# Sparse heads in pairs, values in column halves, early mixer tiles, and three group sums on GpSimd

## What is computed

```
o_sb  = stick_breaking_attention(q_sb, k_sb, v_sb)          # 8 heads
o_dsa = dsa_attention(q_dsa, k_dsa, v_dsa, q_ix, k_ix, w_ix)
        # top 128 keys per query from index scores -> mask
        # p = softmax(q k^T * d^-0.5 + mask), o = p v; k and v are shared by the 8 heads
o = concatenate([o_sb, o_dsa]) @ w_out
x = layer_norm(ALPHA * x + (1 + g_m) * o)
mod = silu(c) @ w_mod + b_mod     # 2 layers x 6 x 1024 columns, in groups of 512 columns
```

## Time and profile before

| | us |
|---|---|
| median of 3 runs | 1759.19 (1757.92 to 1764.79) |
| the profiled execution | 1757.3 |
| its span | 1755.5 |
| PE busy | 1652.4 (94%) |
| DVE busy | 1009.7 (58%) |
| ACT busy | 658.4 (38%) |
| POOL busy | 323.7 (18%) |
| mean granted PE clock | 0.979 |

### The profile page before, as it was taken

How to read it: one execution, slowest core, us unless ns; L and a number is a source line. 1 busy time by engine, 2 the same in 40 slices (tenths; PEclk the granted TensorE clock), 3 DMA queues, 4 the chain that set the end, 5 groups by cost and what they waited for, 6 DMA issues and landing times.

```text
span 1755.5 us, 22795 instructions
## 1 busy us (share of the span) xinstructions
PE 1652.4 (94%) x8957; PEld 1360.5 (77%) x8957; DVE 1009.7 (58%) x1435; ACT 658.4 (38%) x887; POOL 323.7 (18%) x250
## 2 busy tenths in 40 slices
PE   4999999999999997999999999899979899999999
PEld 3798787888777875788887887677757588888887
DVE  3568798777868758533333446757576723333243
ACT  4323465442264523422332123434463533333121
POOL 0000000000000003788885011224301000000011
PEclk8999999999999999999999999999999999999999
DMA  7645200352210332556554332221102133332421
GB/s 277 212 144 192 96 3 1 115 168 96 96 49 25 97 117 97 157 181 189 179 182 160 114 104 79 77 68 64 34 25 75 65 100 96 96 96 90 133 86 48
DMA packets 145606, 187.93 MB, mean 107 GB/s; under 512 B 7054, under 2 KB 104566, under 8 KB 145525
## 3 DMA queue, kind: packets, MB, share of 16 engines
q1 hardware_dynamic: 145524, 186.82, 33.2%
HBM read 184.70 MB, written 2.10 MB: 106 GB/s over the span
## 4 chain that ended last, share of the span: by engine, by line
PE 62%; DVE 13%; POOL 9%; issue 6%; DMA 5%; ACT 3%; SPq 1%; POOLq 0%; DVEq 0%; ACTq 0%
PE ps L841 7%; PE ps L842 7%; PE ps L843 7%; POOL mraw L628 4%; POOL msum L635 4%; DMA mraw<-in_w_mod_dram 3%; PE ps L1343 2%; PE ps L1351 2%; PE ps L1344 2%; PE ps L1347 2%; PE ps L1350 2%; PE ps L1352 2%; PE ps L1406 2%; PE ps L1408 2%; PE ps L1407 2%
## 5 line engine op out<-in xcount | busy, mean ns | idle before, releaser
L1538 ACT ACTIVATE whi<-wraw 128x2048 fp32r<-128x2048 f32 x71 | 135.8, 1913 | 306.3 <-PE ps L843 210.2
L2053 DVE TENSOR_TENSOR wlo<-wraw,whi 128x2048 fp32r<-128x2048 f32 x64 | 148.2, 2315 | 150.6 <-ACT whi L1538 150.4
L2810 DVE TENSOR_TENSOR wlo<-wraw,whi 128x2048 fp32r<-128x2048 f32 x22 | 51.6, 2347 | 204.2 <-ACT whi L1902 204.2
L1343 PE MATMUL ps<-uH,whi 128*128 128x512 f32 x352 | 140.1, 398 | 10.6 <-ACT uH L1870 8.3
L1344 PE MATMUL ps<-uH,wlo 128*128 128x512 f32 x352 | 138.9, 394 | 0.0
L841 PE MATMUL ps<-hH,whi 128*128 128x512 f32 x352 | 138.8, 394 | 0.0
L843 PE MATMUL ps<-hH,wlo 128*128 128x512 f32 x352 | 137.7, 391 | 0.0
L842 PE MATMUL ps<-hL,whi 128*128 128x512 f32 x352 | 137.5, 391 | 0.0
L1350 PE MATMUL ps<-uH,whi 128*128 128x512 f32 x352 | 136.9, 389 | 0.0
L1352 PE MATMUL ps<-uH,wlo 128*128 128x512 f32 x352 | 136.9, 389 | 0.0
L1351 PE MATMUL ps<-uL,whi 128*128 128x512 f32 x352 | 136.9, 389 | 0.0
(11 more groups left out here) (500 smaller groups left out, 3828.8 us busy)
## 6 DMA issues: line engine op xcount, KB each, us to landing
mraw<-in_w_mod_dram SPq DMA_DIRECT2D x104, 512.0 KB, 3.8
wraw<-in_w_gate_dram SPq DMA_DIRECT2D x22, 1024.0 KB, 5.3
wraw<-in_w_up_dram SPq DMA_DIRECT2D x22, 1024.0 KB, 5.4
wraw<-in_w_down_dram SPq DMA_DIRECT2D x16, 1024.0 KB, 5.1
wraw<-in_w_in_dram SPq DMA_DIRECT2D x11, 1024.0 KB, 5.5
mfirst<-in_w_mod_dram SPq DMA_DIRECT2D x16, 512.0 KB, 7.6
wraw<-in_w_in_even_dram SPq DMA_DIRECT2D x8, 1024.0 KB, 5.1
wraw<-in_w_in_odd_dram SPq DMA_DIRECT2D x16, 512.0 KB, 4.6
```

Of the source, the lines that this page charges most:

```text
L1343: mm(o[m], w_[0][m][:, k], uH[:, k], start=(k == 0), stop=False)
L2053: V.tensor_tensor(wlo[:, n % 2, :], wraw[:, n % 2, :], whi[:, n % 2, :].bitcast(F32), ALU.subtract).then_inc(lo_done, 1)
```

## The change

The items run in pairs of heads: item i now has pair `p = i // 8`, query block `q = i // 2 % 4` and head `e = i % 2` of the pair. The turned exponentials of a whole pair are kept, and the values are made once per pair with the values stationary (64 columns) and the exponentials moving, head 0 into partitions 0 to 63 and head 1 into 64 to 127 of one bank. The result lies already turned. The row sums' reciprocals are therefore spread to rows and turned by PE (`factor_rows`), copied by ACT (`factor_copy`) and multiplied in by DVE (`sparse_out`). The four tiles of the stick-breaking heads are turned and split between items. Items with q even are moved by DVE, others by ACT. POOL sums groups 14 to 16. Group 14 is turned after item 14, 15 after 25, 16 in the second chunk of the projection, and with it `sum_group(17)` moves. `sb_values(7)` stands before the wait for the masks.

```
-DSA_TURN = {11: 14, 23: 15}
-DSA_JOB = {2: 1, 8: 2, 14: 3}
-OUT_TURN = {0: 16}
+DSA_TURN = {14: 14, 25: 15}
+DSA_JOB = {2: 1, 8: 2, 17: 3}
+OUT_TURN = {1: 16}
+MIX_TILES = (0, 1, 2, 3, 4, 5, 6, 7)
+SB_TILE = {3: 0, 5: 1, 6: 2, 9: 3}
+TILE_BANK = (2, 7, 2, 7)
+R_TILE = {12: 0, 20: 1, 28: 2}
-G_DVE = (*range(10, 18), 29)
+G_DVE = (10, 11, 12, 13, 17, 29)
...
+        ptdT, = overlay([("ptdT", [P, 2, 2, 13, P], F32)])
...
+            pool.wait_ge(zero_rd, 8)
+            pool.wait_ge(msk_rd, 3)
+            for g_ in range(14, 17):
+                pool.wait_ge(modT, g_)
+                for kp in range(4):
+                    pool.wait_ge(m_landed[kp % 2], 16 * (2 * (g_ - 4) + kp // 2 + 1))
+                    sum_tick(kp, kp % 2, msum_at(g_))
...
-            def dsa_values(i):
-                h, q = i // 4, i % 4
-                pe.wait_ge(dpt_rd[i % 2], i // 2 + 1)
-                if q == 0 and h >= 2:
-                    pe.wait_ge(do_rd, h - 1)
-                for c in range(q + 1):
-                    last = mm(ps[:, 2 + 5 * (h % 2), q * HD:q * HD + HD], ptdT[:, i % 2, c * P:c * P + P],
-                              T0[:, c, DSV:DSV + HD], start=(c == 0), stop=(c == q))
-                last.then_inc(dpv_rd, 1)
+            def dsa_values(p, cs):
+                if cs[0] == 0:
+                    for e in range(2):
+                        pe.wait_ge(dpt_rd[e], 4 * p + 4)
+                    if p < 2:
+                        pe.wait_ge(ao_lo, mixed(2 + p))
+                    else:
+                        pe.wait_ge(do_rd, p - 1)
+                for c in cs:
+                    for e in range(2):
+                        last = mm(ps[e * HD:e * HD + HD, 2 + 5 * (p % 2), c * P:SEQ], T0[:, c, DSV:DSV + HD],
+                                  ptdT[:, p % 2, e, 4 * c:3 * c + 4, :].rearrange("p b n -> p (b n)"),
+                                  start=(c == 0), stop=(c == 3), skip_group_check=True)
...
+            def factor_rows(p):
+                bank = 0 if p == 3 else 3
+                pe.wait_ge(rows_rd, p + 1)
...
+                for q in range(TT):
+                    last = tr(ps[:, bank, q * P:q * P + P], rows_of[:, q * P:q * P + P], ident[:])
+                last.then_inc(aoT, 1)
             pe.wait_ge(wgt_rd, NH - 1)
             dsa_scores(0)
+            dsa_scores(1)
+            sb_values(NH - 1)
             pe.wait_ge(msk_rd, 3)
-            dsa_scores(1)
             dsa_scores(2)
-            sb_values(NH - 1)
-            pe.wait_ge(so_rd, NH)
             for i in range(NS):
                 dsa_turn(i)
+                if i == 2:
+                    pe.wait_ge(so_rd, NH)
                 if i in DSA_JOB:
                     dsa_job(9 + DSA_JOB[i])
                 if i + 3 < NS:
                     dsa_scores(i + 3)
-                if i >= 1:
-                    dsa_values(i - 1)
+                if i >= 8 and i % 8 == 0:
+                    dsa_values(i // 8 - 1, (0, 1, 2, 3))
+                if i in SB_TILE:
+                    sb_tile(SB_TILE[i])
+                if i in R_TILE:
+                    factor_rows(R_TILE[i])
                 if i in DSA_TURN:
-                    pe.wait_ge(job_lo, 10 + sum(at < i for at in DSA_JOB))
+                    pe.wait_ge(fac_copied, 1 if DSA_TURN[i] == 14 else 2)
                     turn_group(DSA_TURN[i])
-            dsa_values(NS - 1)
+            factor_rows(3)
+            dsa_values(3, (0, 1, 2, 3))
...
-            pe.wait_ge(do_rd, NH)
-            mixer_out(0, T0)
             out_product(0, 0, NC1 + 10)
...
             dsa_max(0)
             dsa_max(1)
+            sb_out(NH - 1)
             dsa_max(2)
-            sb_out(NH - 1)
             for i in range(NS):
-                if i % 2 == 0:
+                if on_vector(i):
                     dsa_move(i)
-                if i in DSA_JOB:
-                    dsa_low(DSA_JOB[i])
                 if i + 3 < NS:
                     dsa_max(i + 3)
-                if i >= 4 and i % 4 == 1:
-                    dsa_out(i // 4 - 1)
+                if i - 1 in SB_TILE:
+                    sb_tile_low(SB_TILE[i - 1])
+                if i - 1 in DSA_JOB:
+                    dsa_low(DSA_JOB[i - 1])
+                if i >= 8 and i % 8 == 0:
+                    sum_rows(i // 8 - 1)
+                if i - 1 in R_TILE:
+                    sparse_out(R_TILE[i - 1])
+                if i - 3 in R_TILE:
+                    sparse_low(R_TILE[i - 3])
                 if i - 1 in DSA_TURN:
                     group_columns(DSA_TURN[i - 1])
-                if i < 8:
-                    sum_step(14, i)
-                if 13 <= i < 21:
-                    sum_step(15, i - 13)
-                if i >= 25:
-                    sum_step(16, i - 25)
-            sum_step(16, 7)
-            dsa_out(NH - 1)
+            sum_rows(3)
+            sparse_out(3)
+            sparse_low(3)
```

More of the change, by code:

```diff
@@ L465, in added, with mix_home, mixed, turned_item @@
         def added(g):
-            return ps[:, 3, 256:260] if 14 <= g <= 15 else modp[:, 0:4]
+            return ps[:, 3, 256:260] if 14 <= g <= 15 else (X[:, 2, 0:4] if g == 16 else modp[:, 0:4])
+        rows_of = kid[:, :, :, :].rearrange("p t e d -> p (t e d)")
+        def mix_home(k):
+            if k < 4:
+                slot = (3, 5, 6, 7)[k]
+                return uH[:, slot], uL[:, slot]
+            return (uH[:, 0], uL[:, 0]) if k == 7 else (mixH[:, k - 4], mixL[:, k - 4])
+        def mixed(k):
+            return MIX_TILES.index(k) + 1
+        def turned_item(i):
+            p, q, e = i // 8, i // 2 % 4, i % 2
+            return ptdT[:, p % 2, e, q:4 * q + 1:3, :]
+        def on_vector(i):
+            return i // 2 % 2 == 0
         def sums_bank(g):
@@ L817, in between, with product @@
                     input_tile(15)
-            def product(n, a, nk, u0, xh, xl, w_hi, w_lo, turn=None, k0=0, first=True, done=True, ready=u_lo, near=None, ends=None, mid=None):
+            def product(n, a, nk, u0, xh, xl, w_hi, w_lo, turn=None, k0=0, first=True, done=True, ready=u_lo, near=None, ends=None, mid=None, tiles=None):
                 pe.wait_ge(lo_done, n + 1)
@@ L839, in product @@
                         pe.wait_ge(ready, u0 + k + 1)
+                    if tiles is not None:
+                        k = tiles[k]
+                    x_h, x_l = mix_home(k) if tiles is not None else (xh[:, k0 + k], xl[:, k0 + k])
                     h, l = w_hi[n % 2][:, k, m * P:m * P + P], w_lo[n % 2][:, k, m * P:m * P + P]
-                    mm(o, h, xh[:, k0 + k], start=(first and k == 0), stop=False)
-                    mm(o, h, xl[:, k0 + k], start=False, stop=False)
-                    last = mm(o, l, xh[:, k0 + k], start=False, stop=(done and k == nk - 1))
+                    mm(o, h, x_h, start=(first and first_k), stop=False)
+                    mm(o, h, x_l, start=False, stop=False)
+                    last = mm(o, l, x_h, start=False, stop=(done and last_k))
                     if i == nk - 1 and ends is not None:
@@ L1154, in dsa_job @@
                     pe.wait_ge(mod_rd, 14)
-                if j >= 10:
-                    pe.wait_ge(mod_rd, 14 if j < 12 else 15)
+                if j == 12:
+                    pe.wait_ge(mod_rd, 15)
                 for tt in range(TT):
@@ L1210, in dsa_turn @@
             def dsa_turn(i):
-                q = i % 4
+                q = i // 2 % 4
                 pe.wait_ge(dp_rd, i + 1)
@@ new lines, in sb_tile @@
+            def sb_tile(k):
+                if k == 0:
+                    pe.wait_ge(mod_rd, 14)
+                if k >= 2:
+                    pe.wait_ge(ao_lo, mixed(k - 2))
+                for tt in range(TT):
+                    last = tr(ps[:, TILE_BANK[k], tt * P:tt * P + P], T0[:, tt, k * P:k * P + P], ident[:])
+                last.then_inc(aoT, 1)
+            def factor_rows(p):
+                bank = 0 if p == 3 else 3
+                pe.wait_ge(rows_rd, p + 1)
+                if p == 0:
+                    pe.wait_ge(job_lo, 12)
+                elif p == 1:
+                    pe.wait_ge(job_lo, 13)
+                elif p == 2:
+                    pe.wait_ge(mod_rd, 16)
+                else:
+                    pe.wait_ge(dpt_rd[0], 16)
+                for q in range(TT):
+                    last = tr(ps[:, bank, q * P:q * P + P], rows_of[:, q * P:q * P + P], ident[:])
+                last.then_inc(aoT, 1)
@@ L1318, in out_product @@
                     product(n, use_of(n), KT, 8 * l if not j else None, uH, uL, wT[1], wT[2], turn, ready=ao_lo,
+                            tiles=None if l else MIX_TILES,
                             near=L if j == 2 else None, ends=L if j == 3 else None)
                 moments(L, use_of(n0 + 3))
-            pe.wait_ge(do_rd, NH)
-            mixer_out(0, T0)
             out_product(0, 0, NC1 + 10)
```

88 lines of the change are left out of this document (59 added, 29 removed).

## The result

The changed kernel takes 1768.78 us (median of 10 runs, 1765.51 to 1771.36), the kernel before 1762.15 beside it (median of 10, 1755.58 to 1771.96). The ratio is 1.0041, 95% interval 1.0023 to 1.0059: 7.2 us slower. That lies under the 0.5% named in the prediction, but ten runs of each tell it from no change, it lies outside the forecast range, and it has the other sign. The forecast was taken off 1759.19, the median of three runs of the kernel before; with that base the ratio gives 1766.4, which is outside the range as well.

What follows compares the result with a forecast made beforehand. Bound by PE in the loop, hand-overs at its end, then DVE with POOL in the LayerNorm. Gain 10.8 us, given back 6.8 + 2.0: 2.0 faster, 1759.2 to 1757.2 us; range 1750 to 1765 (own range 1754 to 1761).

Steps and rivals of the forecast that it cites:

- The first turn: Start of the sparse loop: first turn of an item on PE at 573.9 in place of 574.77.
- the values: Sparse loop: both heads' column halves run together, 2.2 us per pair, 8.9 in all; upper bound 17.1.
- the wait at item 25: Sparse loop: PE stands about 3 us for POOL's sum before turning group 15, done at 612.9.
- the shift behind the second chunk: LayerNorm: DVE's later group 17 sum puts the shift 16.2 us after the second projection chunk, 6.8 later than before.
- cold moments: LayerNorm: after a PE pause the moments' products run at the 1.2 GHz level; 2.0 us taken, up to 2.8.
- S: Start of the output projection: 632.17 before, forecast 621.4, so 10.8 us earlier; bounds 617 and 628.
- F: Start of the feed-forward, its first matmul: 688.69 before, 56.5 us after the projection's start.
- Rivals 1 and 2: Sparse loop: column halves don't run together, 1762.8, chance 0.12; POOL stretched to 21.6 per group, 1761.3, chance 0.13.
- rival 3: LayerNorm: smaller delay, group 17's loads landed (4.3 less) and clock stays up (2.0 less): 1750.9; chance 0.20.
- the term of the loop's end: From group 15's turn to the output projection: scores, turns, two tiles, last values and a wait, 8.5 us.
- the 8.8 to be given back in the LayerNorm: After the projection: 6.8 us for the later shift and 2.0 for the low clock.
- The remark on GpSimd: Sparse loop: DVE reads mostly PSUM, so POOL's sums take the undisturbed price, 17.5 us per group.

Runs made afterwards that it cites:

- e2: The changed kernel with group 16 turned in the first projection chunk again, not the second; ratio to the kernel before 0.9977.
- e9: e6 with DVE's copy sb_out(6) put ahead of the last search step of the masks; ratio to before 0.9949, on another chip 0.9962.
- e4: The changed kernel with the spread of pair 3's factors put ahead of the low part of pair 2's tile on DVE; ratio to before 0.9998.
- e5: The changed kernel with the edits of e2 and e4 together; ratio to before 0.9983.
- e6: e5 with group 14 turned after item 11 instead of 14 and the first factor tile moved to item 13; ratio to before 0.9963, run again 0.9947.
- e7: The changed kernel with all value products of one head ahead of the other's, instead of alternating; ratio to before 1.0049.
- e10: e9 with group 16 turned after 12 of the first projection chunk's 16 products instead of 8; 1751.54 us, ratio to before 0.9939.
- the repeats: e6 and e9 run again without further change; ratios to before 0.9947 (e6) and 0.9962 (e9, on another chip).
- e1: The kernel before with only group 16's turn moved to the second projection chunk; ratio to before 1.0044.
- e8: e6 with group 17's sum on GpSimd too; ratio to before 0.9960.
- e3: The changed kernel with only group 14 on GpSimd, DVE summing groups 15 and 16, and group 15 turned after item 23; ratio to before 1.0037.

## Why the prediction was wrong

**Right.** The first turn (573.9 predicted, 573.7 measured), the values (2.2 per pair; 2.37 in three of four blocks), the turn of group 14 (end 594.3 against 593.8), GpSimd's 17.5 us per group (17.4 from 570.59 to 587.96), the wait at item 25 (about 3 us with the turn done at 612.9; 1.78 and 613.0), the shift behind the second chunk (16.2 us predicted, 16.1 measured), cold moments (+2.0; the variance comes 22.3 after the shift instead of 20.0). From S to F the forecast was 65.3 us, measured 65.9. Rivals 1 and 2 did not occur, rival 3 neither. The first turn is in part luck: counted from DVE's copy before it, it comes after 13.6 us in the changed kernel's profile and after 16.1 in that of e2, which is the same program up to there, because the wait shown under e9 is missing in the one and there in the other.

**The step that failed** is the term of the loop's end: "scores 29 to 31 and turns 26 to 31 4.3, two tiles 0.8, last values 2.2, a wait for the last two moves 1.2 ...: 8.5". From 613.0 to 628.4 it took 15.4:

| part | forecast | measured | why |
|---|---|---|---|
| scores and turns | 4.3 | 6.3 | granted clock 0.57 in 614 to 618 |
| two tiles | 0.8 | 1.0 | |
| waits | 1.2 | 4.1 | 0.24, 0.59 and 3.27; the last for DVE's copy |
| last values | 2.2 | 4.0 | low clock behind the wait |
| sum | 8.5 | 15.4 | |

Two things were left out. First, the factor tile of the last pair was put down as a tile of 0.4 us, with no wait for the DVE steps that feed it. But there is one: `factor_rows(3)` stands ahead of the last values in PE's order, and DVE reaches its copy only after the exchange with ACT over the tile before. The prediction asked what DVE does after the last item (the eighth tile, rightly hidden), and not what PE asks of DVE before it. e4 shows it: one exchange in DVE's order, and the wait is 1.0 and the values take 2.37 us. Second, the clock was charged in the LayerNorm alone. But the earlier trace rows show it low (0.73) around a pause at the loop's end as well, and the wait that the prediction itself placed at item 25 has such a stretch behind it: scores and turns take 2.0 us more than forecast. In the profiles with that wait (the changed kernel, e2, e4, e5) the clock falls there, to 0.57 to 0.75 in 614 to 618 us; in those without it (e6, e7 to e10 and the repeats) the scores and turns behind that turn run at 1.00. In e6, where PE doesn't wait there, the way from the turn of group 15 to the projection is 11.6 us, and in e9, where the clock stays up too, it is 10.0. So of the 6.9 us that the term was short, about 1.5 are there even without these two.

With S at 628.4 instead of 621.4, and 0.6 more behind it, the forecast of the feed-forward's start is off by 7.6 us. That is the bulk of the difference in time: forecast −2.0, measured +7.2. The remaining 1.6 are not settled: the stages behind F are the same code, but the way from the feed-forward's first to its last such matmul took 917.7 us in the profile of before and 925.3 in that of after, and between 917.4 and 924.9 in those of the experiments, in no order (921.8 in e1, which has the code of before). So of the 13.2 us between the two profiles, the part behind the feed-forward's start, also 7.6, can't be put down to the change.

**Where the expected gain went**, then: of 10.8 us up to the projection 3.8 came (632.2 to 628.4), the other 7.0 turned into a wait on a queue and two stretches of low clock; and for the 8.8 to be given back in the LayerNorm, 9.4 were.

**The remark on GpSimd.** "DVE reads mostly PSUM in the loop, so I take the undisturbed price": right for POOL, whose groups took 17.4, 18.1 and 17.7 us, and wrong for DVE. The copy L2738 and the low part L2749 work on SBUF alone, and were stretched in every block of the changed kernel; at the loop's end they stand on the path.

## What to carry to other kernels

When a long engine is relieved, follow each of its remaining operands back through the other engine's queue, item by item, at the last item above all: what stands ahead of the producer costs in full there, and a change of order is cheap. Where you expect a wait of TensorE, price the slow stretch behind it as well, as a range: most waits of 1.8 us and more had one here, and some shorter ones did. And a sum moved to GpSimd is a new deadline: after each gain on the path ask again whether it is met (in the first profile of e9 it wasn't, and nearly all of the gain was gone; e10 moved the meeting point by four products and had no wait).

## What the runs showed of the hardware

**DVE beside GpSimd.** A copy from SBUF to SBUF on DVE, and a sum with both operands in SBUF, last until a fixed time after the GpSimd instruction that ran at their start has ended, where that is later than their own length gives. Two steps of the changed kernel with the POOL rows they fall on, in its timelines:

```profile
597.14 0.67 DVE L2738 COPY kid<-small 128x512 f32<-128x512 f32 x1
...
595.92 1.60 POOL L657 TENSOR_TENSOR msum<-mraw 128x512 f32<-128x512 f32 x1
...
595.16 1.23 DVE L2749 TENSOR_TENSOR mixL<-tmp,mixH 128x512 fp32r<-128x512 f32 x1
...
593.95 1.90 POOL L654 TENSOR_TENSOR mraw<-mraw,cpad 128x1024 f32<-128x1024 f32 x1 [5.98 <-PE ps L790]
...
618.61 2.62 POOL L661 TENSOR_TENSOR msum<-msum,mraw 128x512 f32<-128x512 f32 x2
621.30 2.22 POOL L654 TENSOR_TENSOR mraw<-mraw,cpad 128x1024 f32<-128x1024 f32 x1
```

The copy ends at 597.81, 0.29 after POOL's 597.52; the copy of 1.89 us ends at 623.81, 0.29 after 623.52; that of e4 at 624.00, 0.29 after 623.71. The low parts end at 596.39 and 621.77, 0.54 after POOL's 595.85 and 621.23; the near sum of e8 (it adds two rows of `xT`) at 656.77, 0.54 after 656.23. Without GpSimd the copy is 0.43 and the low part 0.68 us (e3). Steps with one operand in PSUM keep their length beside it (L2744 0.68 or 0.69 in all). So such a step lasts for what is left of one GpSimd instruction and 0.29 (copy) or 0.54 us (sum) more; here that made it up to 1.7 us longer (2.38 instead of 0.68, the low part in e4). The Trainium skill states this (SBUF — State Buffer, Who interferes with whom: a VectorE instruction with two SBUF inputs, or a copy in a 2-port mode, contends with GpSimd, and the one that comes second blocks until the other's instruction has ended); the rows agree, as the distances between the ends lie within 0.02 us of each other for each kind.

**Column halves.** The 16 records on two 64-column tiles take 2.37 us with the heads alternating and 3.9 with one after the other (e7). The Trainium skill (TensorE: Matmul & The Clock Gate, Why this matters for your kernels) puts small-M products side by side on distinct column groups; the runs agree, and add that the order of issue decides it. The Trainium skill's rule that a change of tiling mode drains the array (TensorEngine Tiling (Array Packing), Key Properties) would have to lie in the 0.24 us between 2.37 and the 2.13 worked out in the prediction; no run here isolates it.

**The clock.** Waits of 1.8, 2.6 and 3.3 us (at item 25, for group 16 in e9, at the loop's end) were followed by stretches at the low level (a mean of 0.57, 0.66 and 0.83 in windows of 4, 5 and 10 us; records of 512 columns 0.43 apart instead of 0.23). Not every wait of that length was: behind 2.00 us ahead of the product of the near mean (662.61 in the kernel before, 654.60 in e10) and behind 2.56 us at 692.33 in e10 the clock stayed at 1.00. Shorter ones went both ways: behind 1.16 us ahead of group 15's turn in e3 it fell (0.57 in 610 to 614 us), behind 1.2 us for group 16 in e5 it fell too (0.57 in 634 to 638 us), behind that of 1.0 in the repeat of e9 it stayed at 1.00, and behind the 0.59 and 1.0 to 1.2 us at the loop's end the last values ran at full speed in e4, e5, e9 and e10 and slow in e6, e8 and the repeats of e6 and e9. What tells these apart isn't settled by these runs.
